# A fourth width of expert tile, and routing's rank and logits products placed inside its projection

## The reference, cut to what matters

```python
x = x + mixed @ w_out                                  # 2048 x 1024
h2 = rms_norm(x, g_ffn)
logits = h2 @ w_router + b_router                      # 2048 x 32
top_v, top_i = lax.top_k(logits, 4)
gates = softmax(top_v)
# every token goes to its 4 experts: 8192 rows in all
gu = ragged_dot(xs, w_gu, sizes) + b_gu[e_sorted]      # 1024 -> 2048
act = min(gu[:, :1024], 7) * sigmoid(1.702 * min(gu[:, :1024], 7)) * (clip(gu[:, 1024:], -7, 7) + 1)
out = ragged_dot(act, w_down, sizes) + b_down[e_sorted]
x = x.at[tok].add(out * gates)
```

## Time and profile before

| | us |
|---|---|
| median of 3 runs | 5122.44 |
| lowest and highest run | 5120.19, 5128.16 |
| the profiled execution: its own time | 5122.27 |
| its span, first to last instruction | 5120.6 |
| `route`, first to last instruction of the stage | 2052 to 2344 of the span |
| `experts`, from its first transposes on | 2362 to 5100 of the span |
| TensorE busy, whole span | 4948.2 (97%) |
| VectorE, ScalarE, GpSimd busy | 2936.7, 1720.6, 949.9 |
| mean granted TensorE clock | 0.983 of full speed |

### The profile page before, as it was taken

The page is one execution under the profiler, slowest core; times in us unless marked ns, Lnnn a source line. Parts: engine busy times, 40 slices in busy tenths (PEclk is TensorE's granted clock), DMA queues, the critical chain, the costliest instruction groups (busy, mean ns, idle before and its releaser), DMA issues.

```text
span 5120.6 us, 78722 instructions
## 1 busy us (share of the span) xinstructions
PE 4948.2 (97%) x29176; PEld 4406.3 (86%) x29176; DVE 2936.7 (57%) x5669; ACT 1720.6 (34%) x2725; POOL 949.9 (19%) x728
## 2 busy tenths in 40 slices
PE   8999999999799989897999999999999999999998
PEld 7888888888599967776999999999999999999997
DVE  4343332111566785545556666666677777777776
ACT  4121121111266821332333333333344444344443
POOL 0000000232121011222123232132222222212221
PEclk9999999999899999897999999999999999999999
DMA  4222221322644455334446555455466666666665
GB/s 143 103 70 76 83 82 65 134 89 79 200 158 134 150 187 178 131 123 157 152 139 198 172 170 190 160 183 186 153 237 234 234 217 217 215 235 234 229 215 191
DMA packets 261690, 832.41 MB, mean 163 GB/s; under 512 B 34956, under 2 KB 67975, under 8 KB 224008
## 3 DMA queue, kind: packets, MB, share of 16 engines
q1 hardware_dynamic: 226568, 714.75, 39.0%
q0 software_dynamic: 30064, 98.23, 8.0%
q10 hardware_dynamic: 4896, 17.31, 0.9%
HBM read 671.61 MB, written 163.88 MB: 163 GB/s over the span
## 4 chain that ended last, share of the span: by engine, by line
PE 49%; DVE 3%; issue 2%; ACT 0%; POOL 0%; DMA 0%; DVEq 0%; POOLq 0%; ACTq 0%
PE ex_g L2284 32%; PE ex_d L2298 16%; DVE ex_wdl L2391 1%; PE ex_g L2270 1%; DVE ex_xl L2398 1%; ACT ex_xh L2350 0%; DVE ex_at L2421 0%; DVE ex_t L2412 0%; DMA ex_xg<-h_d,ex_nxt 0%; DVE ex_t L2419 0%; DVE ex_ath L2424 0%; POOL ex_y L2238 0%; DVE ex_y L2439 0%; POOL out L2241 0%; DVE ex_wgl L2385 0%
## 5 line engine op out<-in xcount | busy, mean ns | idle before, releaser
L2284 PE MATMUL ex_g<-ex_xh,ex_wgh 128*128 128x256 f32 (+2 forms) x4352 | 1283.6, 295 | 13.7 <-DVE ex_xl L2398 7.4
L2284 PE MATMUL ex_g<-ex_xh,ex_wgl 128*128 128x256 f32 (+2 forms) x4352 | 1277.0, 293 | 0.0
L2284 PE MATMUL ex_g<-ex_xl,ex_wgh 128*128 128x256 f32 (+2 forms) x4352 | 1276.9, 293 | 0.0
L2284 PEld LDWEIGHTS ex_g<-ex_xh,ex_wgh 128*128 128x128 f32 x4352 | 816.5, 188 | 43.8 <-DVE ex_xl L2398 21.9
L2284 PEld LDWEIGHTS ex_g<-ex_xl,ex_wgh 128*128 128x128 f32 x4352 | 816.3, 188 | 7.6
L2284 PEld LDWEIGHTS ex_g<-ex_xh,ex_wgl 128*128 128x128 f32 x4352 | 817.7, 188 | 0.0
L2337 ACT ACTIVATE ex_wgh<-ex_wg 128x2048 fp32r<-128x2048 f32 x274 | 524.5, 1914 | 367.2 <-PE ex_g L2284 340.4
L2385 DVE TENSOR_TENSOR ex_wgl<-ex_wg,ex_wgh 128x2048 fp32r<-128x2048 f32 x274 | 629.0, 2295 | 22.0 <-ACT ex_wgh L2337 16.8
L2238 POOL TENSOR_SCALAR ex_y<-ex_y,ex_cur 128x1024 f32<-128x1024 f32 x82 | 278.7, 3399 | 1529.1 <-DVE ex_y L2439 1529.1
L2298 PE MATMUL ex_d<-ex_wdh,ex_ath 128*128 128x512 f32 x1312 | 523.6, 399 | 0.0
L2298 PE MATMUL ex_d<-ex_wdl,ex_ath 128*128 128x512 f32 x1312 | 515.5, 393 | 0.0
(11 more groups left out here) (378 smaller groups left out, 7688.4 us busy)
## 6 DMA issues: line engine op xcount, KB each, us to landing
ex_wg<-in_w_gu SPq DMA_DIRECT2D x276, 1024.0 KB, 5.1
ex_wd<-in_w_down SPq DMA_DIRECT2D x276, 512.0 KB, 5.9
qkv_d<-prj_o SPq DMA_DIRECT2D x144, 256.0 KB, 2.0
wo_spare<-qkv_d SPq DMA_DIRECT2D x40, 768.0 KB, 4.2
prj_raw<-in_w_in SPq DMA_DIRECT2D x109, 256.0 KB, 3.3
ex_bd<-in_b_down SPq DMA_DIRECT2D x34, 512.0 KB
gate_d<-prj_o SPq DMA_DIRECT2D x64, 256.0 KB, 2.0
mix_ring<-gate_d SPq DMA_DIRECT2D x32, 512.0 KB, 3.8
```

The lines of the kernel that those rows point to most:

```text
L2284: last = pe.matmul(gu[j][:, 0:size], w[:, k, j, :], x[:, k, 0:size], start=(k == 0 and x is xh and w is h), stop=(k == KD - 1 and w is l))
```

## The change

It has two parts. In the experts, a width of 288 slots (NARROW) stands between 320 and 256: an expert with 257 to 288 rows left now gets a tile of 288. The table has one more column, the plan one more range, every engine's stream one more loop and one more value to read. A tile of 288 still has three groups of 128 for the down products, transposes, biases and gathers, as one of 320 has.

In routing, TensorE no longer does `rank` and `logits` behind the second half of the projection but inside it: the ranks before its slice 2, and two slices of the logits before each of its slices 4 to 7 (the bias with the last). VectorE's `split(t + 3)` moves from before the ranks to the end of `choose`, behind the slots and the token number.

The diff, without the lines that only widen a buffer or rename a value:

```diff
-LARGE, MIDDLE, SMALL = 384, 320, 256
+LARGE, MIDDLE, NARROW, SMALL = 384, 320, 288, 256
+SIZES = (LARGE, MIDDLE, NARROW, SMALL)
-TW = 5
+TW = 2 + len(SIZES)
...
-                def project(t, z, h, first=False):
+                def project(t, z, h, first=False, between=None):
...
                     for k in range(KD):
                         if first:
                             pe.wait_ge(wl_ready, k + 1)
+                        if between is not None:
+                            between(k)
...
-                def logits(t):
-                    pe.wait_ge(h2T_ready, 2 * t + 4)
-                    pe.wait_ge(ex_in, t + 1)
-                    for k in range(KD):
+                def logits(t, part=range(KD)):
+                    if part[0] == 0:
+                        pe.wait_ge(h2T_ready, 2 * t + 4)
+                        pe.wait_ge(ex_in, t + 1)
+                    for k in part:
                         pe.matmul(pl[:, 0:NE], h2T[:, k, :], wr[:, k, :], start=(k == 0), stop=False)
-                    pe.matmul(pl[:, 0:NE], ones[0:1, :], br[:, :], start=False, stop=True).then_inc(lg_mm, 1)
+                    if part[-1] == KD - 1:
+                        pe.matmul(pl[:, 0:NE], ones[0:1, :], br[:, :], start=False, stop=True).then_inc(lg_mm, 1)
...
                         project(t + 2, z, 0)
                         turn(t + 1, 1 - z)
-                        project(t + 2, z, 1)
-                        rank(t)
-                        logits(t + 1)
+
+                        def between(k):
+
+                            if k == 2:
+                                rank(t)
+                            if k >= 4:
+                                logits(t + 1, range(2 * (k - 4), 2 * (k - 4) + 2))
+                        project(t + 2, z, 1, between=between)
...
-                    if more:
-                        split(t + 3, 1 - z)
                     dve.wait_ge(rank_mm, t + 1)
...
                     dve.wait_ge(pay_ready, t + 1)
                     chain(tsc(tok[:, :], tok[:, :], float(P), None, ALU.add))
+                    if more:
+                        split(t + 3, 1 - z)
...
-                tsc(middle, cnt[:, :], float(SMALL), None, ALU.is_gt)
+                tsc(narrow, cnt[:, :], float(SMALL), None, ALU.is_gt)
+                tsc(middle, cnt[:, :], float(NARROW), None, ALU.is_gt)
...
+                tt(narrow, narrow, middle, ALU.subtract)
...
+                tsc(third[:, :], ei[:, :], 3.0 * NE, None, ALU.is_ge)
...
+                chain(tt(last_[:, :], last_[:, :], third[:, :], ALU.add))
...
-                for n in (1, 2):
+                for n in range(1, len(SIZES)):
...
-                with pe.Fori(0, n0) as i:
-                    tile(i, LARGE)
-                with pe.Fori(n0, n1) as i:
-                    tile(i, MIDDLE)
-                with pe.Fori(n1, n) as i:
-                    tile(i, SMALL)
+                for k, size in enumerate(SIZES):
+                    with pe.Fori(ends[k - 1] if k else 0, ends[k]) as i:
+                        tile(i, size)
```

More of the change, by code:

```diff
@@ L1794, in route @@
         cnt, two = (t_.sb(n, [P, NE]) for n in ("cnt", "two"))
-        both, upto, before = (t_.sb(n, [P, 3 * NE]) for n in ("both", "upto", "before"))
-        row, ei, nth, second, tail, later, last_ = (t_.sb(n, [P, 1]) for n in (
-            "row", "ei", "nth", "second", "tail", "later", "last"))
+        both, upto, before = (t_.sb(n, [P, len(SIZES) * NE]) for n in ("both", "upto", "before"))
+        row, ei, nth, second, tail, later, third, last_ = (t_.sb(n, [P, 1]) for n in (
+            "row", "ei", "nth", "second", "tail", "later", "third", "last"))
         tab = t_.sb("tab", [P, TW])
@@ L2066, in _ @@
                 dve.wait_ge(cnt_mm, 1)
-                full, middle, small = (both[:, n * NE:(n + 1) * NE] for n in range(3))
-                dve.memset(junk[:, 0:3 * NE], 1.0)
+                full, middle, narrow, small = (both[:, n * NE:(n + 1) * NE] for n in range(len(SIZES)))
+                dve.memset(junk[:, 0:len(SIZES) * NE], 1.0)
                 chain(dve.tensor_copy(cnt[:, :], pr[:, 0:NE]))
@@ L2152, in numbers @@
             eng.wait_ge(tab_in, 16)
-            return (eng.value_load(tab[0:1, 2:3], min_val=1, max_val=NE),
-                    eng.value_load(tab[0:1, 3:4], min_val=2, max_val=2 * NE),
-                    eng.value_load(tab[0:1, 4:5], min_val=3, max_val=2 * NE))
+            return [eng.value_load(tab[0:1, 2 + k:3 + k], min_val=1 + k, max_val=2 * NE) for k in range(len(SIZES))]
         def flat(w):
@@ L2186, in _ @@
                 biases(e)
-                n0, n1, n = numbers(sp)
+                n = numbers(sp)[-1]
                 sp.wait_ge(g_in, 16 * G3)
@@ L2248, in _ @@
                 fetch(0, True)
-                n0, n1, n = numbers(pool)
+                ends = numbers(pool)
                 t_.clear_used(pool)
-                with pool.Fori(0, n0) as i:
-                    tile(i, LARGE // P)
-                with pool.Fori(n0, n1) as i:
-                    tile(i, -(-MIDDLE // P))
-                with pool.Fori(n1, n) as i:
-                    tile(i, SMALL // P)
-                pool.wait_ge(g_in, n * (16 * G3) + 16 * G3)
+                for k, size in enumerate(SIZES):
+                    with pool.Fori(ends[k - 1] if k else 0, ends[k]) as i:
+                        tile(i, -(-size // P))
+                pool.wait_ge(g_in, ends[-1] * (16 * G3) + 16 * G3)
             @block.tensor
@@ L2261, in _ @@
                 pe.sem_inc(down_mm, 1)
-                n0, n1, n = numbers(pe)
+                ends = numbers(pe)
                 def turn(i, b, nb):
@@ L2320, in _ @@
                     turn(0, b, B6)
-                with pe.Fori(0, n0) as i:
-                    tile(i, LARGE)
-                with pe.Fori(n0, n1) as i:
-                    tile(i, MIDDLE)
-                with pe.Fori(n1, n) as i:
-                    tile(i, SMALL)
+                for k, size in enumerate(SIZES):
+                    with pe.Fori(ends[k - 1] if k else 0, ends[k]) as i:
+                        tile(i, size)
             @block.scalar
             def _(act):
-                n0, n1, n = numbers(act)
+                ends = numbers(act)
                 def split_gate_up(i, f, free=None):
@@ L2368, in _ @@
                 split_gate_up(0, 1)
-                with act.Fori(0, n0) as i:
-                    tile(i, LARGE)
-                with act.Fori(n0, n1) as i:
-                    tile(i, MIDDLE)
-                with act.Fori(n1, n) as i:
-                    tile(i, SMALL)
+                for k, size in enumerate(SIZES):
+                    with act.Fori(ends[k - 1] if k else 0, ends[k]) as i:
+                        tile(i, size)
             @block.vector
@@ L2379, in _ @@
                 dve.sem_inc(y_ready, B6)
-                n0, n1, n = numbers(dve)
+                ends = numbers(dve)
                 def split_gate_up(s, z, r):
@@ L2444, in _ @@
                 split_gate_up(1, 1, 1)
-                with dve.Fori(0, n0) as i:
-                    tile(i, LARGE)
-                with dve.Fori(n0, n1) as i:
-                    tile(i, MIDDLE)
-                with dve.Fori(n1, n) as i:
-                    tile(i, SMALL)
+                for k, size in enumerate(SIZES):
+                    with dve.Fori(ends[k - 1] if k else 0, ends[k]) as i:
+                        tile(i, size)
 def hybrid_layer(nc, a, acc_d):
```

4 lines of the change are left out of this document (2 added, 2 removed).

## The result

| | before | changed |
|---|---|---|
| median of the runs, us | 5122.31 (4 runs, 5120.19 to 5128.16) | 5067.05 (4 runs, 5066.52 to 5067.59) |
| span of the profiled execution, us | 5120.6 | 5064.9 |
| routing: first instruction to the experts' first transposes, us | 309.3 (from 2052.4) | 281.3 (from 2055.3) |
| experts: from there to the end, us | 2758.9 | 2728.2 |

The ratio is 0.989 [0.9873, 0.9907]: faster by 55.3 us, where 46.4 were forecast. Both stages of the table were found by their first instructions in the two traces. Routing is 28.0 us shorter, the experts 30.6; the stages ahead of routing, which the change doesn't touch, ended 2.9 us later in this execution. 28.0 + 30.6 - 2.9 = 55.7, the difference of the spans. So the experts came out close to the forecast (31.4), and routing gave nearly twice its 15.0.

The account below looks back on a forecast made before the run. It took TensorE to bound the experts and a loop through four queues, 16.8 us a round, to bound routing. 5122.3 less 31.4 (experts) and 15.0 (routing) gave 5075.9, stated as 5076, range 5062 to 5093.

Parts of the forecast that it names:

- TensorE's floor: Routing, rival: a quicker load lets rounds fall to 14.5 us, where TensorE stops them; 27.6 us saved, 5063; chance 0.17.
- Tiles and widths: Experts: six tiles go from 320 to 288 columns, matmuls 0.1322 us apart, 33.1 us saved.
- The wait that grows: Experts: TensorE waits 0.29 us for VectorE's read of the gate product in each new tile, 1.7 us lost.
- Loop entries and plan, 0: Experts' fourth loop and the plan's extra instructions: both priced at 0, the plan with a bound of 1.2 us.
- Ranks and slots, "about 4.5 us behind h2": Routing: VectorE finishes ranks, slots and token number about 4.5 us behind h2, ahead of the load at 7.7.
- Saved: 12 x 1.20 = 14.4 us: Routing: slots and token number leave the loop behind the split, 1.20 us in each of 12 rounds.
- The tail: Routing's last tile: 0.6 us gained as TensorE's pauses and half clock shrink; bounds 0.9 lost, 1.8 won.
- Routing gives nothing: Routing, rival: scatter issues beside the split slow split or load by 1.2 us a round; 5091; chance 0.2.
- 288 as slow as 320: Experts, rival: 288 columns cost as much as 320, or no expert falls there; 5108; chance 0.04.
- slower by steps of 128: Experts, rival: TensorE takes widths in steps of 128, 288 costs as 384, 67 us lost; 5174; chance 0.03.

Follow-up runs that it names:

- e9: Changed kernel with 290 slots for 288 and VectorE's down-weight split moved behind the step's second read: 5049.88 us, against 5059.04 with 290 slots only.
- e4: Kernel before, with only VectorE's split moved behind the slots and TensorE's order left as it was: 5124.78 us, ratio 1.0001.
- e5b: Changed kernel with GpSimd's scatters held until the residual two tiles on is added, on a second chip: 5075.28 us, against 5066.05 for the changed kernel.
- e5: Changed kernel with GpSimd's scatters held until the residual two tiles on is added, first run: 5072.12 us, ratio 0.9896 to the kernel before.
- e6: Kernel before without routing's scatters, so its output is not right: 5104.16 us, ratio 0.9956.
- e3: Kernel before, with only ranks and logits put inside TensorE's projection and the split left ahead of the ranks: 5123.98 us, ratio 0.9999.

## Why the forecast was right, and which term was off

The sign and the range held, and so did the experts' part. Routing's part didn't: the time came out at 5067, 4 us from the rival called TensorE's floor (5063, chance 0.17) and 9 from the forecast. What came true in routing is the rival, and the range held because it was drawn down to it. By its steps:

- **Tiles and widths.** 6, 5, 3 and 20 tiles as forecast, 0.1317 us for 0.1322, tiles of 87.3 us for 87.2. The six tiles took 6 x (92.46 - 87.33) = 30.8 us less.
- **The wait that grows.** Forecast 0.29 us in each new tile, measured 0.18. The mechanism was right: the products became 0.69 us shorter and VectorE no sooner. What stands ahead of this read is what the forecast named, the bias additions and a split of gate and up weights. It isn't the split of the down weights: e9 moves that one, and the same wait in the first tile of 256 keeps its 0.8 us. At 290 columns no wait is listed here any more.
- **Loop entries and plan, 0.** The first tile of the new loop has the wait of 0.18 us that the others have, and nothing else. The plan's chain got about 1 us longer and none of it shows, for the table is written at 2320.04 and read back at 2322.49, when GpSimd's last scatters have drained (2322.25). The table itself was in memory at 2321.75: half a us more in the plan and it would have been on the path.

```profile
2319.87 0.17 DVE L2126 CAST rt_tab_i<-rt_tab 128x6 int32<-128x6 f32 x1
...
2320.15 0.33 ACTq L1892 DMA_DIRECT2D table_d<-rt_tab_i  x1
2322.49 0.26 SPq L2193 DMA_DIRECT2D ex_tab<-table_d  x1
```

- **Ranks and slots, "about 4.5 us behind h2".** They are done 5.55 us behind it (2172.74 against 2167.19), since VectorE waits 1.50 us for the ranks. It cost nothing: the load comes at 5.9 at the earliest.
- **Routing, the failing term: "Saved: 12 x 1.20 = 14.4 us".** Measured: 12 x (16.77 - 14.57) = 26.4, and with the head and the tail 28.0. Three quantities make the difference. First, the pause of 0.42 to 0.97 us between token number and residual was carried on unchanged ("10.0 and the 0.97 of idle before L1990"), though the forecast called every link of the loop "busy or a DMA". The profile shows nothing that it waited for: as soon as a 1.23 us split is the last instruction ahead of the residual, what the engine does there lies beside it (changed kernel, e4). e5b, in which the load is as slow as before, measures both together: 16.77 - 14.94 = 1.83 us a round, the 1.20 and 0.63 that are left for the pause (its mean over twelve rounds of the kernel before is 0.65). Second, the load: the forecast kept 7.7 us behind h2 and gave the quicker load to the rival with 0.17. e5, e5b and e6 show it as a cause by itself, 1.7 us. Third, the floor: 1.83 + 1.7 would leave a round of 13.2, and TensorE's own work stops it at 14.57, which the rival had put at 14.5. That the whole is TensorE's floor is shown by the rows without idle time.
- **The tail.** Forecast 0.6 us, measured 1.3 from the last of the thirteen h2 to the first transposes of the experts: inside its bounds, and 0.9 of it in the one round that is left. The reason given, that the half clock shrinks with TensorE's pauses, is only half of it, as e6 shows.
- **"Routing gives nothing".** It fell: a scatter's issue beside the split takes 1.62 us instead of 0.97, and the split keeps its 1.23. The Trainium skill (SBUF — State Buffer, SBUF: two separate sides) says that of a VectorE instruction with two SBUF inputs and a GpSimd one that reads SBUF whichever starts first holds the shared ports to its end. The scatter that starts inside the split agrees. The one before it doesn't: it is issued at 2173.37 and runs to 2174.33, and the split starts at 2174.20, right behind ScalarE (2174.17), where by the rule it would have begun 0.13 us later. In another round the split starts 0.02 us into a scatter's 0.97 (2160.09 and 2160.11) and keeps its time. Whether a scatter's record is the time in which it holds the ports, the trace doesn't say.
- **288 as slow as 320, and slower by steps of 128.** Both fell with 295 ns at 288 columns, against 309 at 320, and with 290.

The chances: 0.56 for the forecast was too much against 0.17 for the floor. The argument against the floor was that scatter and load still overlap, the scatter beside the load's end. It rested on a load still 7.7 us behind h2; but a load that has no scatter at its start is in 6.5 us behind h2 on average and 5.9 at the earliest, about when the first scatter goes out (6.2). The load's time was taken as given and the scatter moved against it, while each depends on the other.

## What to carry to other kernels

When a loop closes through several queues, one edit rarely opens it: TensorE's order alone and the split's place alone each gave 0, both together 28 us, since each alone leaves the old loop or makes another one of the same length. Work out the length of every loop through the queues, the engine's own busy time among them, and take the longest one for the new round. And look at what is issued beside a load that the round waits for: taking four small scatters away from it made it 1.7 us quicker, more than the 1.20 us that the edit took out.

## What the runs showed of the hardware

- A product of 224 columns starts 0.1113 us behind the one before, one of 256 0.1179, of 288 0.1317, of 320 0.1466 us. Above 256 the line is nearly straight (13.8 and 14.9 ns for 32 columns), and below it more than half of the gain is lost. The Trainium skill (TensorE: Matmul & The Clock Gate, Back-to-back issue gap) gives the isolated distance a line of one slope, by which an estimated 13.3 ns would be saved below 256 as above it. It adds that the line under-counts at small widths, since the weight load isn't in it, and these rows agree: from 256 to 224 the distance falls by 6.6 ns in the steps shown and by 5.6 on average.
- Four indirect scatters a round, of 128 times 8 bytes each, lengthen a load that starts beside them from 5.4 to 7.1 us, though their queue takes 0.7% of the DMA engines' time there.
- A pause of 0.42 to 0.97 us between two VectorE instructions that wait for nothing in the profile vanishes when the instruction ahead of it is long (1.23 us, in the changed kernel and in e4).
- GpSimd's issue of a scatter gives way to a two-input VectorE instruction that runs already (0.97 to 1.62 us). A split that starts 0.02 to 0.9 us into such an issue isn't held up and keeps its 1.23 us.
- Half clock follows a piece of some 2.5 us of products of 32 columns, with a pause of TensorE behind it (30.7 us of half clock in the middle of routing before, 41.0 in e4) and without one (20.5 in e6, where TensorE never pauses). With that piece broken up there are 6.8 us in e3, behind pauses of 1.3 and 2.1 us, and none in the changed kernel. The round didn't move with it in e3. Where TensorE is itself in the loop, as in e4, it does: 16.8 us with such a stretch and 15.36 without.
